# Three blocks on one core: the weight sums of the last feed-forward layer put in other stages

## The chip, the cores and the metric

The kernel runs on one core of one Trainium2 chip. The metric is the device time of one launch in microseconds (us). All inputs lie in HBM at the start, laid out by the host; the output is written to HBM.

## The reference, cut to what matters

512 tokens of width 1024 go through three layers in float32: a pooling mixer with a convolved feed-forward layer (width 2816), a forgetting attention with a SwiGLU layer, and a state space mixer with a SwiGLU layer.

```python
def reference(x, ...):
    x = first_block(x, c, ctx, ...)      # pooling mixer, then conv_ffn
    return second_block(x, ...)

def second_block(x, ...):
    for i in range(2):
        h = rmsnorm(x, mix_pre_gain[i])
        m = fox_mixer(h, ...) if i == 0 else s5_mixer(h, ...)
        x = x + rmsnorm(m, mix_post_gain[i])
        h = rmsnorm(x, ffn_pre_gain[i])
        x = x + rmsnorm(swiglu(h, ffn_w_gate[i], ffn_w_up[i], ffn_w_down[i]), ffn_post_gain[i])
    return x

def swiglu(h, w_gate, w_up, w_down):
    return (jax.nn.silu(h @ w_gate) * (h @ w_up)) @ w_down
```

The third feed-forward layer is computed with seven instead of eight block products (a scheme in the manner of Strassen and Winograd), for which sums and differences of blocks of its weights are needed. These are the weight sums of the title. They depend on inputs alone, so they can be made at any time before the third up projection reads them.

## The kernel before, in words

**Stages.** TensorE (PE) works through them in this order: start and pooling mixer; first up projection (44 weight slots, from slot S_UP1); first down projection (22, S_DN1); attention, in three parts: values (8 slots, S_V, and the forget logits), heads (24 slots, S_QKG, three to a pair of heads), and output projection (8 slots, S_FO); second up projection (44, S_UP2); second down projection (22, S_DN2); state space stage (8 slots S_S5I, 8 S_GLU, 8 S_S5O); third up projection, partly in pairs (S_UP3, S_PAIRS); products of the third down projection (S_DN3).

**A slot** is 128 x 1024 floats (512 KB) of weights. SyncE's queue (SP) issues the load into `raw`, a ring of five (RING = 5). ScalarE rounds it to `w_hi` (L853), VectorE makes the rest `w_lo` (L1323), and PE runs 24 matmuls in three passes (L2194 to L2196), after which the semaphore `slot_mm` goes up by one. The load of slot n waits until slot n - 5 has been used (`ring_free`). SP is one queue in order: whatever it waits for holds back every load behind it.

**The tables of the state space stage.** In both down projections VectorE, ScalarE and PE make tables for four groups each, in between slots (L1672 to L1727, L1011, L1014, L2370), and SP writes them to HBM in `tables_at` (L689, L692, L694), between weight loads.

**GpSimd (POOL)** does the rest, in program order: after its part in the parameters come `weight_sums` (32 sums, L2163 and L2166), then 16 calls of `turn_tables` (each 40 small operations on POOL, most of which depend on the one before, L2078 to L2096), then `up_sums` (8 steps x 7 chunks = 56 sums, L2179 and L2181), then four small operations of the state space stage (L2189). A sum is a DMA from HBM to HBM, plain or with an addition (`accum_op`), issued from POOL. Each waits for two things: the one before it in the chain (`sum_step`) and a slot of PE (`slot_mm`). `weight_sums(S_UP1 + 22)` begins when 23 slots of the first up projection are used; `up_sums(S_UP2 + 2)` when 3 of the second are.

**The turn tables and SP.** `turn_new` is one buffer. `turn_tables(k)` waits until SP has stored table k - 1 (`turn_out`), and SP stores table k in `turn_store`, right behind the load of head or output slot 2k (counted from S_QKG through S_FO):

```python
def turn_store(n):
    if n % 2 == 0:
        k = n // 2
        sp.wait_ge(turn_new_done, k + 1)
        sp.dma_start(turn_dram[k // 2]...)

for j in range(KT):
    for t, part in enumerate((0, 1, 3)):
        load_fm(S_QKG + 3 * j + t, dram["fox_in"][4 * j + part])
        turn_store(3 * j + t)
```

So the load of slot S_QKG + 1 stands behind table 0, and that of the last output slot, S_FO + 7, behind table 15.

**Readers of the sums.** SP waits for all 88 sums before the pairs of the third up projection (from S_PAIRS), and once more, for the first 32, before the third down projection.

Of the kernel before, what the change touches and what calls it, by code (L numbers as in the profile page):

```python
# [23 lines left out]
KT = D // P  # L24
# [44 lines left out]
S_UP1 = S_POOL + 2  # L69
S_DN1 = S_UP1 + UPS  # L70
S_V = S_DN1 + DNS
S_QKG = S_V + KT
S_FO = S_QKG + 3 * KT
S_UP2 = S_FO + KT
# [8 lines left out]
S_PAIRS = S_UP3 + 2 * PLAIN  # L83
S_DN3 = S_PAIRS + 4 * PAIRED
Y_STEPS = 4 * PAIRED
DOWN_SUMS = 32
SUM_CHUNKS = ((2, 5), (5, 8), (8, 11), (12, 15), (15, 18), (18, 20), (20, 22))
PRODUCTS = 7
PER = FH // 2 + 1
SLOTS = S_DN3 + PRODUCTS * PER  # L90
# [55 lines left out]
def build(nc, dram, out):  # L146
    with ExitStack() as ctx:
# [241 lines left out]
        slot_mm = sem("slot_mm")  # L389
# [107 lines left out]
        sum_step = sem("sum_step")  # L497
# [101 lines left out]
        def _(sp):  # L599
# [216 lines left out]
                for t, src in enumerate(srcs):  # L816
                    sp.dma_start(raw[:, n % RING, T * t:T * t + T], src).then_inc(raw_full[n % RING], 16)

            sp.wait_ge(sum_step, 16 * (DOWN_SUMS + 8 * len(SUM_CHUNKS)))
            for p in range(PAIRED):  # L820
                n, j = S_PAIRS + 4 * p, last_up_tile(PLAIN + p)
                load_halves(n, dram["up3"][2 * j, :, 0:T], v2_v3[0, j])
# [4 lines left out]
                    load_gains(5)  # L827
            q3 = dram["dn3"].rearrange("(q m) p c -> q m p c", q=4)
            sources = (q3[0], v_dram[1], v_dram[2], v_dram[0], v_dram[3], q3[3], q3[2])
            sp.wait_ge(sum_step, 16 * DOWN_SUMS)  # L830
            for i, src in enumerate(sources):
                for s in range(PER):
                    n, k = S_DN3 + PER * i + s, 2 * s
# [1175 lines left out]
        def _(pool):  # L2009
# [144 lines left out]
            def weight_sums(start):  # L2154
                quarter = dram["dn3"].rearrange("(q m) p c -> q m p c", q=4)
                steps = ((0, quarter[0], False), (2, quarter[1], False), (0, quarter[1], True), (2, quarter[3], True),
                         (1, v_dram[0], False), (1, quarter[3], True), (3, v_dram[1], False), (3, quarter[2], True))
                for t, ((to, src, add), m) in enumerate(itertools.product(steps, range(4))):
                    pool.wait_ge(slot_mm, start + t + 1)
                    if t:  # L2160
                        pool.wait_ge(sum_step, 16 * t)
                    if add:
                        pool.dma_start(v_dram[to, m], src[m], max_dma_last_dim=4 * FH * P, accum_op=ALU.add)\  # L2163
                            .then_inc(sum_step, 16)
                    else:
                        pool.dma_start(v_dram[to, m], src[m], max_dma_last_dim=4 * FH * P).then_inc(sum_step, 16)  # L2166
            def up_sums(start):
                gate, val = dram["up3"].rearrange("(j s) p c -> s j p c", s=2)
                lo_k, hi_k = slice(0, T), slice(T, D)
                v4, v1 = v4_v1[:, :, 0], v4_v1[:, :, 1]  # L2170
                steps = ((v4, val[:, :, lo_k], False), (v1, gate[:, :, lo_k], False), (v4, val[:, :, hi_k], True),
                         (v1, val[:, :, lo_k], True), (v2_v3[0], v1, False), (v2_v3[0], val[:, :, hi_k], True),
                         (v2_v3[1], v2_v3[0], False), (v2_v3[1], gate[:, :, hi_k], True))
                for t, ((to, src, add), (j0, j1)) in enumerate(itertools.product(steps, SUM_CHUNKS)):
                    pool.wait_ge(slot_mm, start + t + 1)
                    pool.wait_ge(sum_step, 16 * (DOWN_SUMS + t))
                    dst, src = (a[j0:j1].rearrange("j p c -> p j c") for a in (to, src))
                    if add:
                        pool.dma_start(dst, src, accum_op=ALU.add).then_inc(sum_step, 16)  # L2179
                    else:  # L2180
                        pool.dma_start(dst, src).then_inc(sum_step, 16)  # L2181

            weight_sums(S_UP1 + 22)
            for k in range(PAIRS // 2):
                turn_tables(k)
            up_sums(S_UP2 + 2)
            for i in range(KT):
                pool.wait_ge(yh_done, i + 1)
                pool.tensor_tensor(hl[:, i, :], yfm[:, i, :], hh[:, i, :].bitcast(F32), ALU.subtract).then_inc(y_done, 1)  # L2189
# [746 lines left out]
```

## Time and profile before

| | |
|---|---|
| median of 3 runs | 1724.02 us (1713.88 to 1733.31) |
| profiled execution, its own time | 1720.28 us |
| its span | 1718.2 us |
| mean granted TensorE clock | 0.977 |
| PE busy | 1629.2 us, 95% |
| VectorE (DVE) busy | 1102.5 us, 64% |
| ScalarE (ACT) busy | 724.7 us, 42% |
| GpSimd (POOL) busy | 319.5 us, 19% |
| DMA, mean | 173 GB/s |
| queue of SP (hardware) | 225.44 MB |
| queue of POOL (software) | 62.92 MB |

The profile is of one execution. Times are us from the start of the span. A row of a timeline has the start, the duration, the engine, the line of the kernel, the operation, output and input, shape and count, and in brackets how long the engine stood idle before it and what ended that. Issuing a DMA is not counted as busy time on SP; a sum issued by POOL shows as DMA_DIRECT2D, with the duration of the issue and not of the transfer.

### The profile page before, as it was taken

The numbers are of one execution on the slowest core, as the hardware profiler recorded it, in microseconds if no ns is written. First come the engines' busy times: TensorE is split into PE (matmuls) and PEld (weight loads), VectorE is DVE, ScalarE is ACT, GpSimd is POOL, SyncE is SP. The second block draws the span as 40 slices with busy tenths as digits, with TensorE's granted clock in tenths as the row PEclk, the third lists the DMA queues.
The fourth block names the chain that finished last, engine by engine and source line by source line (L and its number), as shares of the span: only waits on it lengthen the run. The fifth ranks groups of instructions, "written<-read, shape, count | busy, mean of one in ns | idle before, by whom it ended". The sixth has DMA issues, their size and how long they took to land.

```text
span 1718.2 us, 23609 instructions
## 1 busy us (share of the span) xinstructions
PE 1629.2 (95%) x9069; PEld 1379.5 (80%) x9069; DVE 1102.5 (64%) x1774; ACT 724.7 (42%) x1158; POOL 319.5 (19%) x833
## 2 busy tenths in 40 slices
PE   6499999998999999999999999996999999999997
PEld 5378888886877877778888888785888889999786
DVE  6988666665664677756333337564756687777776
ACT  4454433322344767744222222233224444444564
POOL 2011401001307777720111111111011000000000
PEclk8789999999999999999999999998999999999999
DMA  8922257877542222225678878889994235555664
GB/s 354 374 74 99 98 197 193 215 204 214 153 120 83 68 72 71 81 80 172 232 193 182 181 223 208 224 238 247 248 244 122 92 116 183 182 183 184 181 189 145
DMA packets 176961, 297.20 MB, mean 173 GB/s; under 512 B 31713, under 2 KB 115025, under 8 KB 173522
## 3 DMA queue, kind: packets, MB, share of 16 engines
q1 hardware_dynamic: 141842, 225.44, 39.8%
q0 software_dynamic: 20096, 62.92, 16.6%
q10 hardware_dynamic: 14912, 7.34, 1.7%
q8 instruction: 72, 1.18, 0.3%
q14 instruction: 39, 0.32, 0.1%
HBM read 277.84 MB, written 80.73 MB: 209 GB/s over the span
## 4 chain that ended last, share of the span: by engine, by line
PE 74%; DVE 11%; DMA 8%; ACT 3%; issue 2%; SPq 0%; POOL 0%; ACTq 0%; DVEq 0%
PE bank L2194 23%; PE bank L2196 22%; PE bank L2195 22%; DMA raw<-in_dn 3%; DMA u_scratch<-us 2%; DVE ada L1426 2%; DVE w_lo L1323 1%; PE bank L2557 1%; DMA cc<-in_s_c 1%; PE bank L2530 1%; DVE prod L1673 1%; DVE r_tab L1675 1%; DVE r_tab L1672 1%; ACT w_hi L853 1%; PE bank L2686 1%
## 5 line engine op out<-in xcount | busy, mean ns | idle before, releaser
L2194 PE MATMUL bank<-hh,w_hi 128*128 128x512 f32 (+1 forms) x1440 | 521.1, 362 | 7.3 <-DVE w_lo L1323 3.4
L2195 PE MATMUL bank<-hl,w_hi 128*128 128x512 f32 (+1 forms) x1440 | 517.4, 359 | 0.0
L2196 PE MATMUL bank<-hh,w_lo 128*128 128x512 f32 (+1 forms) x1440 | 517.0, 359 | 0.0
L1323 DVE TENSOR_TENSOR w_lo<-raw,w_hi 128x1024 fp32r<-128x1024 f32 x320 | 373.5, 1179 | 210.8 <-ACT w_hi L853 205.7
L853 ACT ACTIVATE w_hi<-raw 128x1024 fp32r<-128x1024 f32 x320 | 325.3, 1021 | 415.4 <-DMA raw<-in_dn 175.4
L2194 PEld LDWEIGHTS bank<-hh,w_hi 128*128 128x128 f32 x1440 | 274.2, 190 | 48.9 <-DVE w_lo L1323 3.8
L2196 PEld LDWEIGHTS bank<-hh,w_lo 128*128 128x128 f32 x1440 | 274.3, 190 | 39.9
L2195 PEld LDWEIGHTS bank<-hl,w_hi 128*128 128x128 f32 x1440 | 274.5, 191 | 39.0
L2194 PE MATMUL bank<-w_hi,hid 128*128 128x512 f32 x352 | 138.6, 394 | 0.9 <-ACT kt L1014 0.9
L2195 PE MATMUL bank<-w_lo,hid 128*128 128x512 f32 x352 | 137.1, 389 | 0.0
L2196 PE MATMUL bank<-w_hi,hid 128*128 128x512 f32 x352 | 137.1, 389 | 0.0
L1484 DVE TENSOR_TENSOR scr<-scr,bank 128x512 f32<-128x512 f32 x22 | 15.1, 688 | 144.8 <-PE bank L2196 144.8
L949 ACT ACTIVATE scr<-bank,convw 128x512 f32<-128x512 f32 x44 | 34.4, 781 | 137.7 <-PE bank L2196 137.7
L2194 PEld LDWEIGHTS bank<-w_hi,hid 128*128 128x128 f32 x352 | 66.2, 188 | 16.9 <-DVE w_lo L1323 1.8
L2196 PEld LDWEIGHTS bank<-w_hi,hid 128*128 128x128 f32 x352 | 66.1, 188 | 13.8
L2195 PEld LDWEIGHTS bank<-w_lo,hid 128*128 128x128 f32 x352 | 66.3, 188 | 13.3
L1459 DVE SCALAR_TENSOR_TENSOR scr<-bank,convw,scr 128x511 f32<-128x511 f32 x44 | 33.0, 749 | 64.4 <-ACT scr L949 64.4
L2179 POOL DMA_DIRECT2D v_v_scratch<-in_up x28 | 33.7, 1203 | 211.1 <-DMA v_v_scratch<-in_up 190.6
L2013 POOL TENSOR_TENSOR turn_new<-turn_t 128x2 f32<-128x2 f32 (+2 forms) x192 | 64.5, 336 | 15.0
L2194 PE MATMUL bank<-m_hi,w_hi 128*128 128x256 f32 x228 | 64.5, 283 | 0.0
L2195 PE MATMUL bank<-m_lo,w_hi 128*128 128x256 f32 x228 | 64.5, 283 | 0.0
L2196 PE MATMUL bank<-m_hi,w_lo 128*128 128x256 f32 x228 | 64.5, 283 | 0.0
(352 smaller groups left out, 2570.6 us busy)
## 6 DMA issues: line engine op xcount, KB each, us to landing
raw<-in_up SPq DMA_DIRECT2D x94, 512.0 KB, 3.8
raw<-in_dn SPq DMA_DIRECT2D x55, 512.0 KB, 5.8
ada<-in_ada_w SPq DMA_DIRECT2D x24, 1024.0 KB, 8.3
v_v_scratch<-in_up POOLq DMA_DIRECT2D x30, 768.0 KB, 7.8
v_scratch<-in_dn POOLq DMA_DIRECT2D x24, 704.0 KB, 6.3
raw<-in_fox_in SPq DMA_DIRECT2D x32, 512.0 KB, 3.5
raw<-in_up SPq DMA_DIRECT2D x57, 256.0 KB, 2.9
raw<-in_s_w SPq DMA_DIRECT2D x24, 512.0 KB, 5.3
```

The source lines that it names most:

```text
L853: act.activation(w_hi[:, n % RING, 0:w], raw[:, n % RING, 0:w], ACT.Copy).then_inc(hi_done, 1)
L949: act.activation(scr[:, 2 * s, :], bank[base + (2 * j + s) % 4][:, :], ACT.Identity, scale=convw[:, j, 4 * s + 1:4 * s + 2], bias=convw[:, ...
L1323: dve.tensor_tensor(w_lo[:, n % RING, 0:w], raw[:, n % RING, 0:w], w_hi[:, n % RING, 0:w].bitcast(F32), ALU.subtract).then_inc(lo_done, 1)
L1426: dot = dve.tensor_tensor_reduce(wt, wt, csil[:, :], 1.0, 0.0, ALU.mult, ALU.add, accum_out=dots[:, m, 2 * b + t:2 * b + t + 1])
L1459: own.add(dve.scalar_tensor_tensor(c[:, 1:T], b[:, 0:T - 1], convw[:, j, 4 * s:4 * s + 1], c[:, 1:T], ALU.mult, ALU.add))
L1672: own.add(dve.tensor_tensor(view, p1, m1, ALU.mult))
L1673: own.add(dve.tensor_tensor(t, p2, m2, ALU.mult))
L2013: own.add(pool.tensor_tensor(out_, a, b, op))
L2179: pool.dma_start(dst, src, accum_op=ALU.add).then_inc(sum_step, 16)
L2194: pe.matmul(dst, w_h, r_h, start=first, stop=False, skip_group_check=True)
L2195: pe.matmul(dst, w_h, r_l, start=False, stop=False, skip_group_check=True)
L2196: return pe.matmul(dst, w_l, r_h, start=False, stop=last, skip_group_check=True)
```

## The change

The sums are issued in another order and other places. The 56 sums for the up projection now come first: 24 in the first up projection, the first when 19 slots are used; 8 in the value part of the attention, one for each slot used; 24 between the 16 turn tables, one after a table of even number and two after one of odd number. The turn tables so come after the 32nd sum; before, they came after the 32nd sum of the other kind. The 32 sums for the down projection follow in the second up projection. No sum is added or dropped, none changes its size, and each still waits for the one before. SP's two waits on `sum_step` follow the new order.

```diff
-DOWN_SUMS = 32
 SUM_CHUNKS = ((2, 5), (5, 8), (8, 11), (12, 15), (15, 18), (18, 20), (20, 22))
+UP_SUMS = 8 * len(SUM_CHUNKS)
@@ SP, before the pairs, and before the third down projection
-            sp.wait_ge(sum_step, 16 * (DOWN_SUMS + 8 * len(SUM_CHUNKS)))
+            sp.wait_ge(sum_step, 16 * UP_SUMS)
...
-            sp.wait_ge(sum_step, 16 * DOWN_SUMS)
+            sp.wait_ge(sum_step, 16 * (UP_SUMS + 32))
@@ POOL, weight_sums
-                    if t:
-                        pool.wait_ge(sum_step, 16 * t)
+                    pool.wait_ge(sum_step, 16 * (UP_SUMS + t))
@@ POOL, up_sums
-            def up_sums(start):
+            def up_sums():
...
-                    pool.wait_ge(slot_mm, start + t + 1)
-                    pool.wait_ge(sum_step, 16 * (DOWN_SUMS + t))
+                    if t:
+                        pool.wait_ge(sum_step, 16 * t)
...
+                    yield
@@ POOL, the order
-            weight_sums(S_UP1 + 22)
+            sums = up_sums()
+            for t in range(24):
+                pool.wait_ge(slot_mm, S_UP1 + 19 + t)
+                next(sums)
+            for t in range(KT):
+                pool.wait_ge(slot_mm, S_V + 1 + t)
+                next(sums)
             for k in range(PAIRS // 2):
                 turn_tables(k)
-            up_sums(S_UP2 + 2)
+                next(sums)
+                if k % 2:
+                    next(sums)
+            assert next(sums, None) is None
+            weight_sums(S_UP2 + 2)
```

## Rows read from the trace of the kernel before

**Rows 1.** The page: the chain that ended last, shares of the span by engine.
```profile
PE 74%; DVE 11%; DMA 8%; ACT 3%; issue 2%; SPq 0%; POOL 0%; ACTq 0%; DVEq 0%
```

**Rows 2.** PE's timeline: rows behind long idle time, outside the start.
```profile
421.80 1.94 PE L2370 MATMUL bank<-ident,r_tab 128*128 128x128 f32 x8 [5.86 <-DVE ya L1344]
...
1106.04 1.94 PE L2370 MATMUL bank<-ident,r_tab 128*128 128x128 f32 x8 [4.15 <-DVE ya L1344]
...
1200.76 2.03 PE L2676 MATMUL bank<-ub,w 128*64 128x64 f32 x32 [8.77 <-DMA ub<-u_scratch]
```

**Rows 3.** Windows: length; busy us (count) of PE, PEld, DVE, ACT, POOL; clock, DMA share, GB/s.
```profile
409.00:429.00 20.00, 14.14 (x82) 11.12 (x81) 13.32 (x21) 1.53 (x3) 2.46 (x3) 0.83 0.76 174
...
1160.00:1220.00 60.00, 43.72 (x319) 37.53 (x318) 32.03 (x61) 17.65 (x30) 5.93 (x5) 0.91 0.98 254
...
801.00:1020.00 219.00, 219.00 (x968) 181.41 (x967) 81.70 (x100) 52.54 (x61) 30.04 (x32) 1.00 0.75 201
...
555.00:745.00 190.00, 189.62 (x1102) 150.63 (x1102) 135.09 (x339) 135.53 (x271) 139.28 (x476) 1.00 0.21 70
```

**Rows 4.** The chain that ended last: a weight load in the first down projection.
```profile
392.36 9.13 DMA raw<-in_dn
```

**Rows 5.** The page: DMA issues, KB each, median us to landing.
```profile
raw<-in_dn SPq DMA_DIRECT2D x55, 512.0 KB, 5.8
```

**Rows 6.** POOL's timeline: down sums 0 and 31; up sums 0, 7, 24, 27, 31.
```profile
223.09 0.78 POOL L2166 DMA_DIRECT2D v_scratch<-in_dn  x1 [30.47 <-PE bank L2196]
...
437.52 0.81 POOL L2163 DMA_DIRECT2D v_scratch<-in_dn  x1 [10.09 <-DMA v_scratch<-in_dn]
...
802.50 0.83 POOL L2181 DMA_DIRECT2D v_v_scratch<-in_up  x1 [55.77 <-PE bank L2196]
...
842.00 0.73 POOL L2181 DMA_DIRECT2D v_v_scratch<-in_up  x1 [3.50 <-DMA v_v_scratch<-in_up]
...
965.20 1.22 POOL L2179 DMA_DIRECT2D v_v_scratch<-in_up  x1 [6.78 <-DMA v_v_scratch<-in_up]
...
991.11 1.14 POOL L2179 DMA_DIRECT2D v_v_scratch<-in_up  x1 [5.39 <-DMA v_v_scratch<-in_up]
...
1018.07 0.73 POOL L2181 DMA_DIRECT2D v_v_scratch<-v_v_scratch  x1 [6.45 <-issue]
```

**Rows 7.** POOL's waits: us in total, times, longest us.
```profile
POOL v_v_scratch L2179 <- DMA v_v_scratch<-in_up: 190.6, 24, 13.0
...
POOL turn_new L2078 <- DMA turn_scratch<-turn_new: 89.7, 15, 56.4
...
POOL v_v_scratch L2181 <- DMA v_v_scratch<-v_v_scratch: 60.8, 11, 7.6
```

**Rows 8.** POOL's timeline: first operation of turn table 1, last of table 15.
```profile
511.16 0.10 POOL L2078 MEMSET turn_new<- 128x2 f32 x1 [56.41 <-DMA turn_scratch<-turn_new]
...
746.36 0.38 POOL L2013 TENSOR_TENSOR turn_new<-turn_t 128x62 f32<-128x62 f32 x1
```

**Rows 9.** SP's waits from 510 to 755 us: total, times, longest us.
```profile
SPq L723 <- POOLq L2096: 73.4, 14, 8.8
```

**Rows 10.** The chain that ended last: the scores of two head pairs in a row.
```profile
569.67 2.18 PE bank L2530 x20
...
594.34 2.18 PE bank L2530 x20
```

**Rows 11.** SP's timeline: loads of S_QKG + 1 and + 2, and of S_FO + 7.
```profile
512.43 5.77 SPq L606 DMA_DIRECT2D raw<-in_fox_in  x2
...
753.72 0.39 SPq L610 DMA_DIRECT2D raw<-in_fox_out  x1
```

**Rows 12.** PE's timeline: value slot 0's second half; S_QKG + 1; first use of S_FO + 7.
```profile
490.34 0.50 PE L2194 MATMUL bank<-w_hi,hh 128*128 128x512 f32 x1
...
539.44 0.39 PE L2194 MATMUL bank<-hh,w_hi 128*128 128x512 f32 x1
...
762.24 0.49 PE L2194 MATMUL bank<-w_hi,vo_hi 128*128 128x512 f32 x1
```

## The prediction, made before the change was run

> **What bounds the kernel now.** I read first the page's chain of the work that ended last: PE holds 74% of the span in it [rows 1], and by the table PE is busy 95%. Only idle time of PE, and time in which its clock is lowered, can be won, and whatever makes PE wait is lost in full. Then I read PE's timeline for its idle time, stage by stage. Apart from the start, the long waits lie in the two down projections (5.86 and 4.15 us, for `ya`) and in the state space stage (8.77 us) [rows 2]. The windows give the clock's part: 1.00 in the long stretches, 0.83 over the 20 us around the first down projection's stall, which is (1 - 0.83) x 20 = 3.4 us of lost work; and at the start of the state space stage PE is busy 43.7 of 60 us at 0.91 [rows 3]. The chain says why PE stands there: in the first down projection it runs through a weight load of 9.13 us [rows 4], where the median lands in 5.8 [rows 5], and from it through ACT and a table's operations on DVE to `ya`. In all three places sums are under way: the down sums run from 223 to 438 us, and the up sums, from 802, at a mean of 6.8 us each, are just over half done at 1018 when the second up projection ends [rows 6]. In the second up projection the same sums cost PE nothing: busy 219.00 of 219 us at a DMA share of 0.75 [rows 3]. So the sums have a price in three stages and none in an up projection; what the values and heads do with them is the question.
>
> **Part one, sums out of the down projections and the state space stage: a gain.** A down projection's chain has two such weight loads one after the other, each ahead of ACT, DVE and the next table. Without sums the first stage saves 9.13 - 5.8 = 3.3 us at one and something less at the other, against an idle time of 5.86, and with it most of the 3.4 us of clock; I take 8. The second saves about as much against 4.15 us idle, so with the same clock 7.6 is all there is; I take 7. Bounds: 2 us each, if the stores of the tables themselves make the loads slow (they are issued just before), and 9.3 and 7.6 if all of it goes. At the start of the state space stage 16.3 us are idle, and its table reads and `ub` transfers stay. I take half, 8, with bounds 2 and 16. Together 23 us (6 to 33).
>
> The 24 sums in the first up projection don't all fit there. Sum 0 may go 4 slots of 5.4 us earlier than 223 us, at 202. The same 24 took 965.2 - 802.5 = 163 us in the second up projection [rows 6], so they end near 365, some 28 us into the first down projection. That is before the stall at 416 to 422 us, so I charge nothing; it is why I don't take all of the 9.3 us there. The 32 down sums took 437.5 - 223.1 = 214 us [rows 6], and the second up projection has 41 slots of 5.4 us = 223 us left after the third: they just fit, at no cost as before.
>
> **Part two, sums in the values and between the turn tables: a loss.** What is queued behind POOL here? A table's end releases SP's turn store, and behind that store stand SP's weight loads. Already before, SP waited at the store for POOL 14 times, 73.4 us in all [rows 9], without stopping PE, since five slots are loaded ahead. The tables had little room: 15 of them took from 511.16 to 746.74 us; of the 89.7 us of waits for the store 56.4 are the first, so 14 waits took 33.3, 2.4 each; a table so takes (235.6 - 33.3)/15 = 13.5 us and the cycle 13.5 + 2.4 = 15.9 [rows 7, 8]. PE takes 24.7 us for the three slots of a head pair [rows 10], 16.5 for two. And table 0, right behind the down sum of 437.5, was ready long before SP came to its store, between the loads of S_QKG and S_QKG + 1 (512.43) [rows 6, 11].
>
> Now, step by step, in the clock of the old trace:
> - Table 0 stands behind sum 31, and sums 24 to 31 start with value slot 0. Its second half starts at 490.3 [rows 12] and is 12 matmuls of 0.227 us, so 493. From sum 24 to 31 the chain took 1018.1 - 965.2 = 52.9 us before [rows 6]. The slots alone allow 36: by the loads from 512.43 on, value slot 7 is used near 528.7, three slots of 5.4 us after slot 4 [rows 11]. The DMA engines are less busy here, so I take 50: table 0 starts at 543 instead of 438.
> - It ends about 12 us later, at 555. The load of S_QKG + 1, which went at 512.43 [rows 11], goes at 556 and is at PE some 6 us later, at 562. PE wanted it at 539.4 [rows 12]: a first stall of 22 us.
> - From there POOL sets the pace. After an even table: one sum is issued, which is hidden in the 2.3 us that the store takes. After an odd table two: the second waits until the first has landed. The waits are 190.6/24 = 7.9 us for an addition and 60.8/11 = 5.5 for a copy [rows 7], with the issue 9.1 and 6.2. Of the seven such places before table 15 three have additions and four copies: 52 us; at the shortest rows of either kind (5.4 and 3.5 us of wait, with the issue 6.5 and 4.2) 36 [rows 6]. The heads' DMA share is 0.21 [rows 3], so I take 44, and 0.5 us each to start the table, 47.5. The eight even places take 8 x 2.3 = 18.4.
> - The tables: 13.5 us each beside a DVE that is busy 135 of 190 us [rows 3]. DVE's same work is now spread over a longer stretch, so I take 12.7. The bound from above is 13.5; from below 11, a little under POOL's own busy time for one (139.28/190 x 15.9 = 11.7) [rows 3]. 16 x 12.7 = 203.
> - Table 15 ends at 543 + 203 + 47.5 + 18.4 = 812, not 747. The load of S_FO + 7 follows 0.6 us later. Before it went at 753.72 and was used at 762.24 [rows 11, 12], 8.5 us; with less beside it I take 7. PE is at 819.6 where it was at 762.2: 57.4 us late. That holds the first 22 us and does not add to them. The clock falls once more near the end: 2 us, on the 3.4 of either stall [rows 3]. In sum 59 us.
>
> Bounds of this part: 20 us, where only the first stall is left (sums as fast as the slots, tables at 11 us: then table 15 ends near 770), and 83 us (tables at 13.5, all sums as slow as before, a chain of 55).
>
> The Trainium skill, page "DMA: Bandwidth & Descriptors", section "Anatomy of one DMA — SWDGE (gpsimd) path", fits a DMA from GpSimd as 2.0 us and the bytes at 436 GB/s, 3.8 us for a sum of 768 KB by that estimate. This case's trace does not agree: no wait for an addition ended in under 5.4 us. By the page's figures the seven double places would cost 7 x (3.8 + 0.5) = 30 us, not 47.5.
>
> **The sum.** The profiled execution took 1720.3 us. 1720.3 + 59 - 23 = 1756. The runs' median is 1724.0, 3.7 above that execution, so the median after is 1760.
>
> **The rivals.**
> - *The sums land fast in a stage with idle DMA engines.* For it: DMA share 0.21 in the heads against 0.75 and more where the sums were timed [rows 3]. Then the value part is paced by slots (table 0 at 529), the seven double places cost 36 + 3.5 = 40 us, as at the shortest rows, and table 15 ends at 529 + 203 + 40 + 18 = 790; PE is 790 + 7.6 - 762 = 36 us late, and 36 - 23 = +13: 1737. Against it: the chain of 24 has a mean of 6.8 us, and the shortest rows are single ones. Chance 0.15, with PE 20 to 38 us late. The page's fit, above, points the same way and further, 10 us less, 1727.
> - *The sums are slower beside DVE than before*, or tables slower because POOL issues in between: cost above 78 us, net over +60, near 1795. For it: the issue and the tables share POOL, and a table's small operations took longer where DVE was busy. Chance 0.10.
> - *Faster: POOL stays off the path.* The mechanism is the ring: SP may be late by as much as is loaded ahead. Its place is the load of S_QKG + 1, and it decides if table 0 is done before 533 us (539.4 less 6), against my 555. Then only the gain is left, -23 us: 1724 - 23 = 1701. Against it: POOL may not start the table before value slot 7 is used at 528.7, and a table takes 11 us at the least, so 540 is the earliest; only a faster chain of later tables could then hold the loss under the gain. Chance 0.06.
> - *The change does nothing* for the down projections, because the table stores and not the sums make the loads slow. Then the gain is 6 and not 23: 1760 + 17 = 1777. It is inside my range, chance 0.15 within the forecast.
>
> **How the numbers follow.** The forecast, table 15 some 55 to 80 us later than before, has 0.69; the rivals 0.15, 0.10 and 0.06. Its own range is a net of +15 to +60, 1739 to 1784. The range to hold 8 in 10 reaches into the two next cases: 1733 to 1790. About 1%, 17 us, is what a measurement of this kernel can tell from no change. Slower by more than that needs a net over +17: nearly all of the forecast and the slow rival, 0.80. Within 1%: the fast rival and a low end of the forecast, 0.15. Faster: 0.05.
>
> **What the profile after would show.** Right: the first L2078 near 540 us; idle time of PE before matmuls on head and output slots, put down to `w_lo`, 50 us or more in total; SP's wait at L723 for POOL several times 73.4 us; the starts of the tables in turns 15 and 20 us apart; weight loads in the second down projection landing in 6 us or less, and PE's 4.15 us there gone; no sum after the second up projection. Wrong: table 15 ending before 775, or PE busy without gaps through the heads. The prediction would be wrong by the size of the sums' time in the heads first, and by the down projections' gain second.

## The result: 2.75% slower, as forecast in kind and nearly in size

| | before | after |
|---|---|---|
| median of 4 runs each | 1720.65 us | 1769.21 us (1765.33 to 1774.5) |
| ratio | | 1.0275, 95% interval 1.0207 to 1.0344 |
| profiled execution, span | 1718.2 us | 1763.6 us |
| PE busy | 1629.2 us | 1634.2 us |
| mean granted clock | 0.977 | 0.968 |

The medians are 48.6 us apart, the spans of the two profiles 45.4; the forecast was +36 us. PE has the same 9069 matmuls. Of the 45.4 us, 40 are idle time that came on balance, and 5 are longer busy time of the same matmuls, beside a lower granted clock. The page of the kernel after: the chain that ended last, by engine (before: [rows 1]).

```profile
PE 64%; POOL 10%; DMA 10%; DVE 9%; issue 4%; ACT 2%; SPq 0%; ACTq 0%; POOLq 0%; DVEq 0%; PEldq 0%
```

GpSimd (POOL), which held nothing of the chain before, now holds 10% of it. SP's waits from 495 to 830 us (before: [rows 9], 73.4 us):

```profile
SPq L723 <- POOLq L2096: 295.0, 16, 49.1
SPq L606 <- PE bank L2206: 10.5, 4, 4.7
```

SP, which used to wait for ring slots that PE had to free, now waits for turn tables. PE's timeline: the transposes of the tables in the first down projection, the longest idle times in the heads and the output projection (before, none of 2 us stood in this stretch), and the state space stage:

```profile
413.86 1.07 PE L2380 MATMUL bank<-ident,r_tab 128*128 128x128 f32 x8 [0.91 <-DVE ya L1344]
...
553.76 0.80 PE L2204 MATMUL bank<-hh,w_hi 128*128 128x512 f32 x1 [24.60 <-DVE w_lo L1323]
565.65 0.79 PE L2581 MATMUL bank<-sq_hi,blk64r 128*128 128x512 f32 x1 [5.52 <-DVE sq_lo L1786]
...
589.99 0.79 PE L2514 MATMUL bank<-qk 64*128 64x512 f32 x2 [9.14 <-DVE qk L1798]
...
669.97 0.80 PE L2581 MATMUL bank<-sq_hi,blk64r 128*128 128x512 f32 x1 [7.20 <-DVE qf L1788]
...
829.63 0.80 PE L2204 MATMUL bank<-w_hi,vo_hi 128*128 128x512 f32 x1 [9.20 <-DVE w_lo L1323]
...
1251.13 1.20 PE L2686 MATMUL bank<-ub,w 128*64 128x64 f32 x32 [1.94 <-DMA ub<-u_scratch]
```

One stall of 24.6 us before S_QKG + 1, then shorter ones wherever a table was late. (The last, at 829.63, is for the load of S_FO + 6, which went at 814.06, behind table 14, and landed 13.2 us later.) The 5.86 us before the transposes at 421.80 are 0.91 here, those before 1106.04 are gone, and the 8.77 us in the state space stage are 1.94 [rows 2].

**Where the time went, by marks on PE's timeline.** A mark is a matmul that both kernels run once, at the end of a stage or near it. Two of the kernel before are in [rows 12]: 490.34 in the values and 762.24 in the output projection. The marks of after:

```profile
479.88 0.50 PE L2204 MATMUL bank<-w_hi,hh 128*128 128x512 f32 x1
...
832.35 0.77 PE L2204 MATMUL bank<-w_hi,vo_hi 128*128 128x512 f32 x1
...
1197.24 1.03 PE L2380 MATMUL bank<-ident,r_tab 128*128 128x128 f32 x8
...
1420.92 1.32 PE L2244 MATMUL bank<-ident,htok 128*128 128x128 f32 x8 [0.19 <-DVE htok L1410]
```

and the last two of before, which were not shown yet:

```profile
1133.54 1.03 PE L2370 MATMUL bank<-ident,r_tab 128*128 128x128 f32 x8
...
1375.22 1.32 PE L2234 MATMUL bank<-ident,htok 128*128 128x128 f32 x8 [0.15 <-DVE htok L1410]
```

| stretch, ended by the mark | before | after | shift | gained or lost | forecast |
|---|---|---|---|---|---|
| start to the values (slot 0, second half) | 490.34 | 479.88 | -10.5 | -10.5 (0.7 of it before 90 us) | -8 |
| values, heads, output slots (first use of S_FO + 7) | 762.24 | 832.35 | +70.1 | +80.6 | +59 |
| to the last table's transposes, second down projection | 1133.54 | 1197.24 | +63.7 | -6.4 | -7 |
| to the last transposes before the third up projection | 1375.22 | 1420.92 | +45.7 | -18.0 | -8 |
| to the end | 1718.2 | 1763.6 | +45.4 | -0.3 | 0 |

Leaving three stages, the sums gave back 34 us (9.8, 6.4 and 18.0). Where they went they cost 81. The table is of one profile of each kernel. The 18.0 of its fourth line are not all the state space stage: 6.5 of them lie ahead of the last transposes of the second down projection (1178.01 before, 1235.22 after), where the kernel before stood 3.4 and 1.9 us, and 11.5 behind them. And the first line is less sure than it looks: experiment e4 (below) is the kernel before up to its first turn table, and its profile reached the first mark 4.8 us sooner.

```profile
485.55 0.50 PE L2195 MATMUL bank<-w_hi,hh 128*128 128x512 f32 x1
```

### The profile page after: what moved, and what is told of

The parts are those of the page before. It is cut to its first block, busy times and chain, and to the rows that moved or that the text cites. A ratio compares the mean times of both kernels' runs of the same rounds, so it can differ in the third digit from the quotient of the medians.

```text
span 1763.6 us, 23585 instructions
## 1 busy us (share of the span) xinstructions
PE 1634.2 (93%) x9069; PEld 1384.4 (78%) x9069; DVE 1101.6 (62%) x1774; ACT 725.9 (41%) x1158; POOL 306.3 (17%) x833
## 4 chain that ended last, share of the span: by engine, by line
PE 64%; POOL 10%; DMA 10%; DVE 9%; issue 4%; ACT 2%; SPq 0%; ACTq 0%; POOLq 0%; DVEq 0%; PEldq 0%
PE bank L2204 20%; PE bank L2206 20%; PE bank L2205 20%; POOL turn_new L2013 4%; POOL turn_t L2013 2%; DMA v_v_scratch<-v_v_scratch 2%; DMA v_v_scratch<-in_up 2%; DVE ada L1426 2%; POOL turn_t L2090 2%; POOL turn_t L2093 2%; DMA raw<-in_dn 1%; DVE w_lo L1323 1%; DMA turn_scratch<-turn_new 1%; DMA raw<-in_fox_out 1%; DVE htok L1410 1%
## 5 line engine op out<-in xcount | busy, mean ns | idle before, releaser
L2204 PE MATMUL bank<-hh,w_hi 128*128 128x512 f32 (+1 forms) x1440 | 524.0, 364 | 28.6 <-DVE w_lo L1323 24.6
L2204 PEld LDWEIGHTS bank<-hh,w_hi 128*128 128x128 f32 x1440 | 275.5, 191 | 71.4 <-DVE w_lo L1323 25.2
L1459 DVE SCALAR_TENSOR_TENSOR scr<-bank,convw,scr 128x511 f32<-128x511 f32 x44 | 32.9, 748 | 64.3 <-ACT scr L949 64.3
```

Of the source, the lines that this page charges most:

```text
L1459: own.add(dve.scalar_tensor_tensor(c[:, 1:T], b[:, 0:T - 1], convw[:, j, 4 * s:4 * s + 1], c[:, 1:T], ALU.mult, ALU.add))
L2204: pe.matmul(dst, w_h, r_h, start=first, stop=False, skip_group_check=True)
```

## The experiments

Each is the changed kernel with the edit shown, unless it says otherwise. All kernels compute the whole reference. The mark "S_FO + 7" is PE's first use of that slot, the one behind table 15. The medians of the kernel before, taken anew beside each group of experiments, are 1720.7, 1723.1, 1721.4 and 1724.3 us, so a difference between kernels of two groups is uncertain by some 3 us.

### 1 and 2. What sets the pace of the heads

```diff
 e1_single
                 turn_tables(k)
                 next(sums)
-                if k % 2:
-                    next(sums)
+            for t in range(8):
+                next(sums)
 e2_table0_first
+            turn_tables(0)
             for t in range(KT):
                 pool.wait_ge(slot_mm, S_V + 1 + t)
...
-                turn_tables(k)
+                if k:
+                    turn_tables(k)
 e3_table0_single: both edits
 e9_quiet_heads
                 turn_tables(k)
+            for t in range(24):
                 next(sums)
-                if k % 2:
-                    next(sums)
```

> The changed kernel, but with one sum behind each turn table instead of one and two in turns; the 8 that are left follow table 15. Theory (POOL's own chain sets the pace of the heads, and its excess is the second sum, which waits for the first): the gaps after odd tables, 6.95 to 11.35 us and 62.7 in all, fall to 2.3 each, table 15 ends 47 us earlier, at about 778, and so does everything behind it: 1769 - 47 = 1722 us. Rival (the pace is set by something that both kernels share: the late table 0, or the DMA traffic of the sums beside the weight loads, which stays): 1760 to 1770 us.

> The changed kernel, but with turn table 0 made before the 8 sums of the value part instead of behind them. The stall of 24.6 us before S_QKG + 1 goes in either theory. Theory (only the end of table 15 counts): the chain from sum 31 on is shorter by one table and one store wait, 10.1 + 2.3 = 12.4 us: 1769 - 12 = 1757 us; the stall moves to later slots. Rival (each stall counts for itself): 1769 - 25 = 1744 us.

> Both edits together: table 0 before the sums of the values, one sum behind each table. Theory: table 15 ends 47 + 12 = 59 us earlier than in the changed kernel, near 766, where the kernel before had 747 and PE's need, moved by the gain of the first down projection, lies near 743: some 20 us of loss stay, of which the 35 us won in other stages make a gain on the kernel before: 1769 - 59 = 1710 us. Rival (the 8 sums left over, now in the second up projection with the 32 others, spill into the second down projection and take back 5 to 10 us): 1715 to 1720 us.

> The changed kernel with all 24 sums of the heads moved behind table 15. Table 0 stays behind the 8 sums of the values. It is for its trace up to S_FO + 7, not for its time: 56 sums now follow, through the second down projection into the state space stage, as in the kernel before. Theory (after one sum per table, what is left of the loss is the late table 0 and PE's own work behind it): S_FO + 7 is used near 800, as with one sum per table (802.5), where it was 832 in the changed kernel. Rival (each single sum between tables costs its issue, 1 us or more): 785 to 790.

| | time, us | S_FO + 7 | first long stall |
|---|---|---|---|
| before | 1723.1 (16 runs) | 762.2 | none |
| changed | 1769.2 | 832.4 | 24.6 us at 553.8 |
| e1: one sum per table | 1737.1 (7 runs) | 802.5 | 25.2 us at 557.5 |
| e2: table 0 first | 1762.1 (4 runs) | 824.9 | 29.9 us at 567.9 |
| e3: both | 1728.3 (10 runs) | 789.0 | 30.1 us at 567.9 |
| e9: no sum in the heads | 1748.9 (1 run) | 800.7 | 24.0 us at 554.9 |

Taking out the second sums won 32 us, so the rival of e1, a pace set by something that stays, falls. But it won 32 and not 47, and the working of that expectation was too simple. POOL's own chain got only 34 us shorter: table 15 ended at 790.7 us, where it had ended at 824.8 and I had said 778. The first table began 3.8 us later, and the sixteen tables together took 216 us instead of 206. The 206 are the odd ones: in the kernel before, in e4 and in e9, where the heads hold no sums, the tables took 219, 216 and 215. In the changed kernel DVE has the same work beside them in a longer stretch (170.8 us busy in 352, in e1 in 320, by the windows below); that this is why they are shorter there is argued and not shown. The window of e1 from 592 to 790 us:

```profile
592.00:790.00 198.00, 198.00 (x1127) 157.07 (x1126) 136.98 (x341) 134.89 (x270) 160.02 (x504) 0.99 0.42 114
```

PE is busy 198 of 198 us: in this stretch PE is the bound, and POOL runs just ahead of it. The load of S_FO + 7 then waited 2.1 us for a ring slot and landed in 7.3 us. What is left of the loss is what PE lost before 592. From the mark in the values to S_FO + 7 the kernel before, the changed one and e1:

```profile
490.34:762.24 271.90, 268.19 (x1442) 214.15 (x1442) 170.71 (x386) 165.82 (x313) 174.11 (x600) 1.00 0.26 83
```

```profile
479.88:832.35 352.47, 283.92 (x1442) 224.98 (x1443) 170.77 (x386) 166.19 (x313) 205.92 (x671) 0.91 0.49 126
```

```profile
483.02:802.54 319.52, 279.05 (x1443) 221.64 (x1443) 170.82 (x386) 165.69 (x313) 210.70 (x665) 0.93 0.47 126
```

e1 needs 47.6 us more than the kernel before for the same matmuls: 36.8 us of idle time, nearly all in four stalls before 592 (25.15, 5.08, 3.08 and 5.82 us), and 10.9 us of longer busy time, at a mean clock of 0.93 instead of 1.00. It had been 7.3 us ahead at the first mark, so it comes to S_FO + 7 40 us late. The finish is the later of two paths, POOL's tables in a row and PE's own work behind its stalls; the second sums had made POOL's the later one, and without them the two end within some 4 us of each other.

e9 says what a single sum behind a table costs: nothing. Without any sum in the heads S_FO + 7 comes at 800.7, with sixteen single ones at 802.5. POOL's own chain shows the same: from its first table to the end of table 15 it took 249.9 us without sums and 250.9 with sixteen. (The time of e9, 1749 us, is one run and not to be compared: its sums run into the later stages.) The rival, an issue of 1 us per sum, is out: the issue lies in the 2.3 us in which the table's store lands.

e2 told between the end of table 15 and the stalls one by one. The first stall did not go. It moved behind the load of S_QKG + 3, which stands behind table 1, and was 29.9 us long; both the theory and the rival had it vanish or wander cheaply. Table 1 could start only once sum 32 was issued behind the value sums, at 544.5 (548.3 in the changed kernel). The time moved by 7 us, S_FO + 7 by 7.5; the end of table 15 (its store went at 817.5 instead of 824.9) moved by as much. So the end of table 15 counts, as the theory had it, and the length of the first stall does not; the 12.4 us were too many, and the rival's 1744 us is out. e3 against e1 says much the same: 8.8 us in the time and 13.5 at S_FO + 7. e3 fell 18 us short of the 1710 that I expected, and the largest part is that of e1: its table 15 ended at 777.6 and not near 766. Its rival, a spill of the 8 sums left over, named 1715 to 1720 and does not reach 1728 either. Against the kernel before, e1 is 0.9% slower (ratio 1.0085, 1.0055 to 1.0116) and e3 level with it (1.0026, 1.0002 to 1.0049).

### 3. A late table 0 alone, and two by two alone

e4 is the kernel before with one wait more; e10 is e5 (below) with the second sums put back.

```diff
 e4_late_table0 (the kernel before)
+            pool.wait_ge(slot_mm, S_V + 8)
             for k in range(PAIRS // 2):
                 turn_tables(k)
 e10_early_two (e5)
                 turn_tables(k)
                 next(sums)
+                if k % 2:
+                    next(sums)
-            for t in range(8):
-                next(sums)
```

> The kernel before, with one more wait: POOL starts turn table 0 when value slot 7 is used (528.7 us) instead of at 438. No sum is moved, none lies between the tables. Theory: 16 tables of 13.2 us and 15 store waits of 2.3 in a row end at 529 + 211 + 35 = 775, so PE is at S_FO + 7 at 782 instead of 762: 1721 + 20 = 1741 us. Rival (only the first stall counts): table 0 ends near 540, S_QKG + 1 is at PE near 547 instead of 539: 1721 + 8 = 1729 us. Second rival (five loaded slots hide it): 1721 us.

> e5_early, but with one and two sums behind the turn tables in turns, as in the changed kernel; none is left over behind table 15. Table 0 is early, so the two by two alone are priced. Theory (seven second sums of 9 us instead of a store wait of 2.3, so POOL's chain of tables 1 to 15 lasts 195 + 16 + 63 = 274 us from 505 on and ends near 779 instead of 745; the ring and PE's slack of 0.6 us per table take some): S_FO + 7 near 787 instead of 759, 1695 + 28 = 1723 us. Rival (without the late table 0 the loaded slots absorb the second sums): 1695 to 1702 us.

e4: 1748.2 us (4 runs) against 1723.1, ratio 1.0134 (1.0095 to 1.0173); S_FO + 7 at 785.8 instead of 762.2, where the theory had 782. No sum was touched, and by starting one table 86 us later, at 524.0, S_FO + 7 comes 23.5 us later; counted from the mark in the values, which this profile reached 4.8 us early, 28.3 us are lost. The stall before S_QKG + 1 is 6.3 us only, and three of 3 to 6 us follow: both rivals (8 us, or none) fall. Table 15 ended at 774.8, where the theory had 775.

e10: 1726.7 us (10 runs) against 1695.4 for e5, 31 us more (29 by the ratios to the kernel before, 1.0004 and 0.9834); S_FO + 7 at 795.1 against 759.0. The theory had 1723 and 787, the rival 1702 at the most. POOL's waits in e10 from 500 to 790 us:

```profile
POOL v_v_scratch L2167 <- DMA v_v_scratch<-in_up: 27.3, 4, 8.9
POOL v_v_scratch L2169 <- DMA v_v_scratch<-v_v_scratch: 17.6, 3, 6.3
...
POOL v_v_scratch L2167 <- DMA v_v_scratch<-v_v_scratch: 3.5, 1, 3.5
```

These are 48.4 us; 1.7 of them lie behind table 15, the rest is seven waits of a second sum for the first, 6.7 us each (3.5 to 8.9), with nothing else out of place. Counted by where S_FO + 7 comes, late table 0 with single sums (e1) is 43.5 us behind e5, the second sums alone (e10) 36.1, and both together, the changed kernel, 73.3, which is 6 us less than the sum of the two.

### 4. A placement that beats both, and the price of sums by stage

```diff
 e5_early
+            for t in range(4):
+                pool.wait_ge(slot_mm, S_UP1 + 1 + t)
+                next(sums)
             s5_parameters()          # and in it, ahead of its second wait for ScalarE:
+                for t in range(4):
+                    pool.wait_ge(slot_mm, S_UP1 + 7 + t)
+                    next(sums)
...
-            for t in range(KT):
-                pool.wait_ge(slot_mm, S_V + 1 + t)
-                next(sums)
             for k in range(PAIRS // 2):
                 turn_tables(k)
                 next(sums)
-                if k % 2:
-                    next(sums)
+            for t in range(8):
+                next(sums)
 e6_early_ssm, on top of it, in weight_sums
-                    pool.wait_ge(slot_mm, start + t + 1)
+                    pool.wait_ge(slot_mm, start + t + 1 if t < 24 else S_S5I - TAIL + 1)
 e7_early_dn2, on top of e5
+                    pool.wait_ge(slot_mm, start + t + 1 if t < 16 else S_DN2 + 2 + (t - 16))
 e8_early_big, on top of e5: the last four of the eight steps in larger chunks, 44 up sums
+BIG_CHUNKS = ((2, 7), (7, 11), (12, 17), (17, 22))
...
-            for t in range(24):
+            for t in range(20):
                 pool.wait_ge(slot_mm, S_UP1 + 19 + t)
...
-            for t in range(8):
-                next(sums)
```

> The same 88 sums, placed by what the runs showed: 4 up sums from the first slot of the first up projection on, 4 more in the waits of POOL's parameters, 24 as in the changed kernel, none in the values, one behind each of the 16 turn tables (table 0 comes right behind sum 31, so before the values), 8 and the 32 down sums in the second up projection. Theory (a sum costs only where it delays a turn table or lies in a down projection or the state space stage): no stall in the heads, the gains of the changed kernel kept, 9.8 + 7 + 18 us: 1721 - 35 = 1686, with a spill of the last sums into the second down projection up to 1692 us. Rival (a single sum between tables costs too, since a table with its store takes 15.9 us of PE's 16.5: 16 issues of 1 us): 1700 to 1710 us.

> e5_early, but the last 8 down sums wait for the start of the state space stage; all else stays. It prices the sums in that stage alone. Theory (the 18 us which the changed kernel was quicker there came from its missing sums): e5_early + 15 to 20 us, with ub and u_scratch transfers of 8 us and more. Rival (the stage is limited by its own table reads, as the prediction assumed for half of it): + 8 us or less.

> e5_early, but the last 16 down sums are paced by the slots of the second down projection. It prices the sums there alone. Theory (weight loads behind the table stores land late beside a sum, and PE waits for ya): e5_early + 7 us, with PE idle 3 to 5 us before a table's transposes and the clock at about 0.83 around it. Rival (the clock and the idle time come from the table stores alone): + 0 to 2 us.

> e5_early, but the last four of the eight steps of the up sums are made in 4 chunks of 1 and 1.25 MB instead of 7 of 512 and 768 KB: 44 up sums, none left over for the second up projection. Theory (a sum moves at a rate of its own, hardly set by other traffic: 768 KB in about 8 us): landings of 11 to 13 us in the heads, still inside the table's 15.9 us, and the time that of e5_early or up to 5 us less. Rival (most of a sum's time is fixed): landings below 9 us.

| | time, us | ratio to before (1721.4) |
|---|---|---|
| e5 | 1695.4 (4 runs, 1686 to 1703) | 0.9834 (0.9777 to 0.9891) |
| e6: 8 sums in the state space stage | 1710.0 (8 runs) | 0.9913 (0.9882 to 0.9944) |
| e7: 16 sums in the second down projection | 1702.3 (4 runs) | 0.9880 (0.9835 to 0.9925) |
| e8: larger chunks | 1693.8 (4 runs, 1692.7 to 1694.9) | 0.9825 (0.9773 to 0.9877) |

e5 keeps every sum and is 26 us faster than the kernel before (1.7%, with an interval clear of 1), and 74 faster than the changed one. Its profile is of its slowest run, 1703.3 us, 8 above the median, so its trace shows it at its worst. It falls short of 1686: S_FO + 7 comes at 759.0, where the kernel before, moved by the 10.5 us that the changed kernel had won by then, would have it at 752. The rival, a price for single sums, falls with e9. In this profile the first down projection gained less (its last transposes came at 480.95, before at 487.61), and a wait of 2.1 us in the output slots is left.

Eight sums in the state space stage cost 14.6 us by the medians, near the theory (15 to 20) and far from the rival's 8 or less; the intervals of the two ratios overlap by 0.0009, and the traces below bear the price out. The window over its start, e6 and then e5, shows where:

```profile
1165.00:1225.00 60.00, 50.55 (x389) 43.84 (x388) 32.99 (x74) 12.71 (x16) 4.30 (x6) 0.89 0.93 252
```

```profile
1165.00:1225.00 60.00, 57.28 (x497) 49.82 (x496) 39.77 (x90) 18.49 (x24) 0.00 (x0) 0.97 0.81 225
```

PE is idle 9.5 us instead of 2.7, at a clock of 0.89 instead of 0.97. The transfers between the `us` and `ub` tiles and HBM land in 7.2 us at the median in e6, as in the kernel before (the theory had 8 and more), and in 4.3 in e5 (4.5 in the changed kernel).

Sixteen sums in the second down projection cost 6.9 us by the medians, as the theory had it, but not at the place that it named: no wait for `ya` over 0.9 us is left in e7, and the clock near its tables is 1.00; its waits are 1.2 us at 1142.6 and 3.0 at the last transposes, at 1171.2. The intervals of e5 and e7 overlap, and e5's runs spread over 17 us, so the medians alone do not shut out the rival's 0 to 2 us. The traces do. From the last transposes of the output projection to those of the second down projection, e7 and then e6, which has no sums there:

```profile
788.35 1.32 PE L2247 MATMUL bank<-ident,htok 128*128 128x128 f32 x8 [3.06 <-DVE htok L1410]
...
1171.19 1.78 PE L2247 MATMUL bank<-ident,htok 128*128 128x128 f32 x8 [3.04 <-DVE htok L1410]
```

```profile
787.00 1.32 PE L2247 MATMUL bank<-ident,htok 128*128 128x128 f32 x8 [0.92 <-DVE htok L1410]
...
1163.23 1.32 PE L2247 MATMUL bank<-ident,htok 128*128 128x128 f32 x8 [0.25 <-DVE htok L1410]
```

That is 382.8 us against 376.2. The same marks in all twelve profiles give the price of the sums by stage, us:

| stretch | with down or up sums in it | without |
|---|---|---|
| start to the mark in the values | 490.3 (before), 485.6 (e4) | 479.9 to 483.0 (changed, e1, e2, e3, e9) |
| last transposes of the output projection to those of the second down projection | 389.8 (before), 385.7 (e4), 384.7 (e9), 382.8 (e7) | 376.2 to 377.7 (the other eight) |
| from there to the last transposes before the third up projection | 197.2 (before), 208.0 (e4), 203.6 (e6) | 185.3 to 190.7 (the other nine) |

(In the first line, "without" means that the sums end near 365 us; e5 to e8 and e10, whose sums run to some 405 us, are between, 481.9 to 484.9.) In each stage every profile with sums is longer than every one without. In the first stage the distance is 2.5 us at the least and 10.5 at the most.

e8: DMA issues of the larger sums (output and input, queue, operation, KB each, median us to landing), and then those of e5:

```profile
v_v_scratch<-v_v_scratch POOLq DMA_DIRECT2D x6, 1280.0 KB, 7.2
v_v_scratch<-in_up POOLq DMA_DIRECT2D x6, 1280.0 KB, 12.1
```

```profile
v_v_scratch<-in_up POOLq DMA_DIRECT2D x30, 768.0 KB, 8.0
...
v_v_scratch<-v_v_scratch POOLq DMA_DIRECT2D x10, 768.0 KB, 5.4
```

The additions of 1280 KB land in 12.1 us, as the theory had it. The copies land in 7.2, below the 11 to 13 of the theory and inside what the rival named (under 9), so the theory holds for the additions alone. From 768 to 1280 KB a copy takes 1.8 us more, and an addition some 4 (the 8.0 us of the 30 sums from `in_up` are a median over 20 additions and 10 copies). How much of a sum's time does not depend on its size can't be read from these rows: the four copies of 512 KB in e5 took longer than those of 768.

```profile
v_v_scratch<-v_v_scratch POOLq DMA_DIRECT2D x4, 512.0 KB, 6.6
```

The time of e8 is that of e5, with runs 2 us apart instead of 17.

## Why the prediction was right, and where it was off

**The mechanism** held at each step. POOL's tables are queued behind the value sums, SP's loads behind the tables. Table 0 began at 536.0; with the 10.5 us that the stages before had gained, that is 546 in the clock of the old trace, and I had said 543. It ended after 10 us, where I had said 12. S_QKG + 1 was at PE 14.3 us later than before by the clock, 24.8 with the shift; the forecast was 22. The eight even places took 18.3 us, and the forecast was 18.4. From the load of S_FO + 7 at 825.46 to its use at 832.35 it took 6.9 us, the forecast 7.

**The term of the heads was 59 us and measured 80.6.** Its largest miss is the seven double places, between the end of an odd table and the start of the next: 47.5 us forecast, 64.3 measured (the expectation of e1 has 62.7). Of these, 55.2 lie between the issues of the two sums. I had lowered the 52 us of the old trace to 44, because the DMA engines were less busy in the heads. POOL's timeline after, the second sums of tables 3, 5 and 7:

```profile
604.30 1.23 POOL L2178 DMA_DIRECT2D v_v_scratch<-in_up  x1 [7.52 <-DMA v_v_scratch<-in_up]
...
646.30 1.13 POOL L2178 DMA_DIRECT2D v_v_scratch<-in_up  x1 [8.40 <-DMA v_v_scratch<-in_up]
...
682.23 0.73 POOL L2180 DMA_DIRECT2D v_v_scratch<-v_v_scratch  x1 [5.80 <-DMA v_v_scratch<-v_v_scratch]
```

In the heads an addition is waited for 7.5 to 9.0 us and a copy 5.1 to 6.6. Against sums of the same size, 768 KB, in the second up projection of the kernel before, at a share of 0.75, the additions are not shorter (8.3 us at the mean of three against 7.7 of ten), nor are the copies (6.2 of two against 5.2 of twelve). The step that failed is the reading of the DMA share. The 0.21 of the old trace, and the 0.46 of the new one (window below), are means over the heads, and a sum does not run beside the mean. The end of an odd table releases SP's turn store and two weight loads together with the sum. Three of the seven places after, each from the issue of the first sum to that of the second, have shares of 0.92, 0.80 and 0.81:

```profile
595.50:604.30 8.80, 8.80 (x40) 7.27 (x39) 6.55 (x24) 6.05 (x16) 1.28 (x2) 0.99 0.92 216
636.60:646.30 9.70, 6.84 (x45) 4.51 (x45) 4.43 (x7) 4.63 (x5) 1.29 (x2) 1.00 0.80 203
675.60:682.20 6.60, 6.60 (x55) 4.45 (x54) 4.15 (x9) 1.88 (x2) 0.81 (x1) 1.00 0.81 292
```

The DMA engines were as busy beside these sums as in the second up projection. What a sum would take with idle engines beside it no run shows. The shortest rows on which I built the lower bound were also of sums of 512 KB, and at five of the seven places the sum waited for is one of 768. Besides, POOL stands 0.56 us between the last operation of a table and the issue of a sum, and the issue of the second sum holds it 0.7 us more before the next table: 1.3 us a place, where I had taken 0.5. The sixteen tables took 12.9 us each and not 12.7, 3 us together. The value sums took 52 us and not 50, and table 0 so began 3.5 us later than I had said. With the shift of 10.5 us that is the end of table 15: at 824.8 and not at 812 less 10.5, 23 us later. What the clock did adds nothing to this term. Over the heads and output slots it was 0.93, and from mark to mark PE was busy 15.7 us longer for the same matmuls (the windows above: 283.92 against 268.19); but the rest of the weights of S_FO + 7, `w_lo`, were ready only at 832.3 us, by way of a load that stood behind table 15, and at full clock PE would have waited for them instead.

```profile
831.04 1.23 DVE L1323 TENSOR_TENSOR w_lo<-raw,w_hi 128x1024 fp32r<-128x1024 f32 x1 [1.47 <-ACT w_hi L853]
```

The 2 us that I had added for the clock were not there at that mark. The window of the heads and output slots:

```profile
555.00:825.00 270.00, 230.69 (x1218) 181.60 (x1217) 154.83 (x365) 152.60 (x294) 182.38 (x595) 0.93 0.46 121
```

**The gain of the state space stage was 8 us and measured 18**, above my upper bound of 16 for it. The 16.3 us of idle time from which I took half are of a window that starts at 1160, inside the second down projection, as the 18 do; 11.5 of the 18 are the stage itself. I had taken half because its own table reads and `ub` transfers stay. They do, but they were slow because of the sums (7.2 us, and 4.5 without), which e6 shows by putting eight sums back: 14.6 us. With the idle time the lowered clock of 0.91 went too, and I had not priced it there, though I had in the down projections. The same work after, 57.5 of 60 us busy at a clock of 1.00:

```profile
1217.00:1277.00 60.00, 57.50 (x445) 49.53 (x443) 44.38 (x89) 24.00 (x41) 0.00 (x0) 1.00 0.80 231
```

The terms of the down projections, 15 us together, measured 16.2 (9.8 and 6.4). For the first that is in part this pair of profiles: by all of them the gain there is 2.5 to 10.5 us.

The two misses, 22 us too little loss and 10 us too little gain, partly cancelled. That is luck: 1760 was nearer to 1769 than its terms deserved. The 80.6 us even lie above the 78 from which I had priced the slow rival, sums slower than before in the heads. Half of that rival came true: the second sums took somewhat longer than those in the second up projection, though the tables did not (12.9 us against 13.5). Only the larger gains elsewhere kept the net, 48.6, inside the forecast's own range of 15 to 60.

**The rival of fast sums** had POOL's waits shrink where DMA engines are idle. Its time and its 20 to 38 us at S_FO + 7 are out: the loss was 70, and in e10 each second sum waited 6.7 us. Its condition was never met, since the engines were not idle beside those sums. The Trainium skill, page "DMA: Bandwidth & Descriptors", section "Anatomy of one DMA — SWDGE (gpsimd) path", would give 3.8 us for 768 KB by an estimate from its fit; the measured ones are 5.4 for a copy and about 8 for an addition, so that the trace does not agree. My sentence that no wait for an addition ended in under 5.4 us was not right: in the kernel before the sum at 1099.50 waited 5.0 us for an addition of 512 KB. For 768 KB none took under 6.6.

**The rival of a POOL off the path** can be had, but not by this placement: e5 and e8 are it, with an early table 0 and no second sum, and they are 1.7% faster than the kernel before (0.9834 and 0.9825, both intervals clear of 1).

## What to carry to other kernels

A move of work off a contended stage has two prices, what it frees and what it now stands in front of. Here the queue that took the work in (POOL's) released a wait in another queue (SP's), behind which stood all weight loads, and the slack of that path was readable beforehand: 15.9 us needed of every 16.5. Where such a loop has less slack than one transfer, put one transfer per turn where a store's landing hides it, never two that wait for each other. And take the traffic beside a transfer from the window in which it will run, not from the mean of its stage: what releases the transfer may release others with it.

## What was not expected of the hardware

- A stage with a low mean DMA share can be full at the moments that count: 0.46 over the heads after, 0.80 to 0.92 in three windows of its second sums, and additions of 768 KB took 8.3 us there against 7.7 in a stage at 0.75. Beside the fullest traffic they took longest: in the kernel before, from 1133 to 1220 us at a share of 0.97, five such additions were waited for 10.3 us at the mean, 7.3 to 13.0.

```profile
1157.16 1.26 POOL L2179 DMA_DIRECT2D v_v_scratch<-in_up  x1 [12.99 <-DMA v_v_scratch<-in_up]
```

- Smaller transfers on ScalarE's queue in the state space stage do get slower beside the sums: `u_scratch` and `ub`, 256 KB each, 4.5 us without and 7.2 with.
- A turn table, 40 small dependent operations on POOL, took 10.0 us with DVE idle (table 0 after, PE stalled) and 16.7 before with DVE busy for 9.5 of them; in the heads 12.9 (after) and 13.5 (before) at the mean. PE, ScalarE and the DMA engines were busier in the long one too, so which of them the difference comes from is not shown. In the windows, table 0 before and after:

```profile
438.05:454.75 16.70, 16.70 (x102) 13.80 (x101) 9.49 (x16) 2.21 (x3) 14.81 (x41) 1.00 0.69 167
```

```profile
536.00:546.00 10.00, 0.00 (x0) 0.00 (x0) 0.00 (x0) 0.00 (x0) 8.07 (x41) 0.50 0.24 79
```

- A long stall costs more than itself. In the 24.6 us without matmuls the granted clock fell to the lower level (0.50 in the window above, 1.2 of 2.4 GHz). The first nine matmuls behind it, from 553.76 us, started 0.43 to 0.59 us apart, and from 558.14 on they started 0.23 us apart; after the next stall, of 5.5 us, they stood 0.43 us apart again.

```profile
555.21 0.63 PE L2204 MATMUL bank<-hh,w_hi 128*128 128x512 f32 x1
555.63 0.63 PE L2205 MATMUL bank<-hl,w_hi 128*128 128x512 f32 x1
...
558.61 0.39 PE L2204 MATMUL bank<-hh,w_hi 128*128 128x512 f32 x1
558.83 0.39 PE L2205 MATMUL bank<-hl,w_hi 128*128 128x512 f32 x1
```
